# Conditioning weights by input rows, input tiles in three banks, low parts on GpSimd

## The reference, cut to what matters

```
mod = silu(c) @ ada_w + ada_b                      # ada_w 1024 x 6144, c: 9 rows
sh1, sc1, g1, sh2, sc2, g2 = split(mod, 6)
h = rms_norm(x) * (1 + sc1) + sh1
z = h @ w_in                                        # 1024 x 1792
u_pool, v_conv, g_conv, x_lru, g_lru = split(z)
o_pool = pool_mixer(u_pool)                         # running means, then a 64 x 64 product per group
o_conv = silu(layer_norm(depthwise_conv31(v_conv * sigmoid(g_conv))))
xc = conv4(x_lru); r, i = sigmoid(xc @ wa + ba), sigmoid(xc @ wx + bx)
a = exp(-8 r softplus(-lam)); s = scan(a, sqrt(1 - a^2) * i * xc); o_lru = s * gelu(g_lru)
x = x + g1 * (concat(o_pool, o_conv, o_lru) @ w_out)
h2 = rms_norm(x) * (1 + sc2) + sh2
x = x + g2 * moe(h2)                                # top 4 of 32 experts, three 1024 x 1024 matrices each
y = rms_norm(x)
```

## Time and profile before

| | us |
|---|---|
| median of 3 runs (lowest to highest) | 1331.99 (1330.03 to 1334.34) |
| the profiled execution, its time | 1334.82 |
| its span, first to last instruction | 1333.0 |
| PE busy, share of the span | 1251.9 (94%) |
| DVE, ACT, POOL busy | 284.1, 193.0, 118.8 |
| chain that ended last: PE, DMA, DVE, SP's queue | 81%, 8%, 5%, 3% |
| the experts' products, line 1941, share of that chain | 61% |

### The profile page before, as it was taken

How to read it: one execution, slowest core, us unless ns; L and a number is a source line. 1 busy time by engine, 2 the same in 40 slices (tenths; PEclk the granted TensorE clock), 3 DMA queues, 4 the chain that set the end, 5 groups by cost and what they waited for, 6 DMA issues and landing times.

```text
span 1333.0 us, 18761 instructions
## 1 busy us (share of the span) xinstructions
PE 1251.9 (94%) x7974; PEld 551.4 (41%) x7974; DVE 284.1 (21%) x562; ACT 193.0 (14%) x331; POOL 118.8 (9%) x178
## 2 busy tenths in 40 slices
PE   5889979959999999999999999999999999999976
PEld 2758847723333333333333333333333333333322
DVE  2643874673010000010000000001010010001027
ACT  3515251210000000000000000000001001000021
POOL 2011042010100000000001000000000001000000
PEclk9989979959999999999999999999999999999978
DMA  9647278399999999999999999999999999999973
GB/s 362 188 130 254 95 280 272 152 398 386 359 422 421 420 421 422 409 408 410 417 410 420 421 415 420 421 420 394 415 422 419 422 421 421 421 422 421 421 293 151
DMA packets 92004, 486.42 MB, mean 365 GB/s; under 512 B 13649, under 2 KB 21852, under 8 KB 41206
## 3 DMA queue, kind: packets, MB, share of 16 engines
q1 hardware_dynamic: 82451, 462.04, 86.3%
q0 software_dynamic: 8608, 20.82, 4.2%
q10 hardware_dynamic: 859, 2.32, 0.4%
HBM read 470.26 MB, written 18.04 MB: 366 GB/s over the span
## 4 chain that ended last, share of the span: by engine, by line
PE 81%; DMA 8%; DVE 5%; SPq 3%; ACT 1%; issue 1%; POOL 1%; ACTq 0%; DVEq 0%; POOLq 0%
PE psum L1941 61%; DMA raw<-in_moe_w_down 4%; PE psum L1593 4%; PE psum L1588 2%; PE psum L1589 2%; PE psum L1590 2%; SPq L518 2%; PE psum L1931 2%; PE psum L1760 1%; DMA cvs<-in_conv_dw 1%; PE psum L1656 1%; PE psum L2062 1%; DMA raw<-in_ada_w 1%; PE psum L1935 1%; POOL w_lo L687 1%
## 5 line engine op out<-in xcount | busy, mean ns | idle before, releaser
L1941 PE MATMUL psum<-raw,aT 128*64 128x512 f32 (+1 forms) x1728 | 301.2, 533 | 5.1 <-DMA raw<-in_moe_w_down 5.0
L1941 PE MATMUL psum<-raw,xb 128*64 128x512 f32 (+1 forms) x1920 | 304.6, 514 | 0.0
L1941 PE MATMUL psum<-raw,xa 128*64 128x512 f32 x1280 | 283.5, 595 | 0.0
L1514 DVE TENSOR_SCALAR act_t<-psum 128x512 f32<-128x512 f32 (+1 forms) x46 | 28.4, 642 | 874.7 <-PE psum L1941 874.7
L1941 PEld LDWEIGHTS psum<-raw,xb 128*64 128x64 f32 (+1 forms) x1920 | 100.6, 126 | 189.1 <-issue 176.7
L1941 PEld LDWEIGHTS psum<-raw,aT 128*64 128x64 f32 (+1 forms) x1728 | 98.3, 129 | 188.9 <-issue 166.7
L1941 PEld LDWEIGHTS psum<-raw,xa 128*64 128x64 f32 x1280 | 88.2, 137 | 169.7 <-issue 169.4
L701 POOL DMA_INDIRECT xrow<-h_scratch,gidx x24 | 27.4, 1143 | 464.1 <-PE psum L1593 430.0
L999 ACT ACTIVATE glu<-psum 128x512 f32<-128x512 f32 (+1 forms) x46 | 24.3, 559 | 291.8 <-PE psum L1941 291.8
L1588 PE MATMUL psum<-hT_hi,w_hi 128*128 128x260 f32 x208 | 59.4, 285 | 0.0
L1589 PE MATMUL psum<-hT_lo,w_hi 128*128 128x260 f32 x208 | 58.9, 283 | 0.0
(11 more groups left out here) (403 smaller groups left out, 912.6 us busy)
## 6 DMA issues: line engine op xcount, KB each, us to landing
raw<-in_moe_w_gate SPq DMA_DIRECT2D x128, 1024.0 KB, 26.2
raw<-in_moe_w_up SPq DMA_DIRECT2D x128, 1024.0 KB, 26.4
raw<-in_moe_w_down SPq DMA_DIRECT2D x128, 1024.0 KB, 27.1
raw<-in_ada_w SPq DMA_DIRECT2D x24, 1024.0 KB, 7.6
raw<-in_w_in SPq DMA_DIRECT2D x7, 1024.0 KB, 12.4
x<-in_x_prompt SPq DMA_DIRECT2D x2, 2048.0 KB
raw<-in_w_out SPq DMA_DIRECT2D x4, 1024.0 KB, 12.8
yrow_a<-y_scratch SPq DMA_DIRECT2D x2, 2048.0 KB, 10.6
```

The costliest lines, as they stand in the source:

```text
L1514: v.tensor_scalar(act_t[:, b, 0:bank.shape[1]], bank, 8.0, -6.0, ALU.min, ALU.max).then_inc(u_done, 1)
L1941: last = mm(out[w * g4:w * g4 + w, :], x, weights[:, 8 * w * g4:8 * w * g4 + 8 * w], start=start, stop=stop)
```

## The change

A mod chunk is now 128 input rows by 2048 columns, so that each partition reads one run of 8 KB instead of four runs of 2 KB. Eight chunks make one half (g1 and sh2, then 1 + sc2 and g2), which is summed in bank 3, in four strips of 32 partitions, over the whole time of those eight chunks. The 16 chunks are spread between all input tiles, where before 4 came after the fourth pair and 12 after the last. The results leave in two steps, one a half, with eight DMAs of 2 KB rows instead of 32. The input tiles use banks 0 to 2, two neighbours sharing bank 1, where before two pairs took banks 0 to 3. The gates 0 and 1 stand right behind the convolution, in front of the fourth pair of tiles. `lru_out` becomes `lru_mul`, which only multiplies; the high parts of all eight output tiles are made at the end, and the low parts of five of them and of three chunks of `w_out` by POOL (before: two chunks, no output tiles). `ng2` moves into `adab` as 2 loads instead of 8.

```diff
-USE = ([("ada", i) for i in range(ADA_A)] + [("in", i) for i in range(4)] + [("mod", i) for i in range(4)]
...
+USE = (span_of("ada", 0, ADA_A) + span_of("in", 0, 3) + span_of("mod", 0, 4) + span_of("in", 3, 1) + span_of("mod", 4, 4)
...
@@ SP
+            load_piece("mod", 0)
+            sp.wait_ge(zeroed, 2)
...
+            load_piece("mod", 1)
+            for q in range(2):
+                load_late(ng2[32 * q:32 * q + 32, :], norm2_g[:, 512 * q:512 * q + 512].to_broadcast([32, 512]))
+            load_piece("mod", 2)
             sp.wait_ge(mix_done, 1)
@@ POOL
-            for n in range(8):
-                if n in (4, 5):
-                    g.wait_ge(ada_sc, n - 3)
-                else:
-                    g.wait_ge(ada_ev, 5 + n if n < 4 else 3 + n)
+            for h in range(2):
+                g.wait_ge(ada_ev, 5 + h)
+                if h:
+                    g.wait_ge(ada_sc, 1)
                 for j in range(4):
...
+                    g.dma_start(mod_d[:, q], modst[32 * j:32 * j + NC, :]).then_inc(mod_out[h], 16)
-            for c in C_OUT[2:4]:
+            def lo(c):
...
+            lo(C_OUT[0])
+            lo(C_OUT[1])
+            for i, (kk, src) in enumerate(POOL_SPLITS):
+                g.wait_ge(o_hi, i + 1)
+                g.tensor_tensor(oT[:, :, 1, kk, :], by_tile(src)[0], oT[:, :, 0, kk, :].bitcast(F32), ALU.subtract)\
+                    .then_inc(o_split, 1)
+            lo(C_OUT[3])
@@ ACT
+            gates(0)
+            gates(1)
+            roots(0)
+            roots(1)
+            evict(3, (0,))
...
             evict(6)
             gates(2)
             gates(3)
             roots(2)
             roots(3)
             hi(C_OUT[0])
+            mod_rows(1)
             hi(C_OUT[1])
             hi(C_OUT[2])
             hi(C_OUT[3])
@@ DVE
+            lru_mul(2)
+            lru_mul(3)
+            scale_rows()
+            lo(C_OUT[2])
+            dve.wait_ge(lru_made, 4)
+            dve.wait_ge(pool_in, 2)
+            for kk, src in POOL_SPLITS[0:4]:
+                o_high(kk, src, src[:, SEQ:TOK])
+            for m in range(4):
+                o_high(4 + m, x_lru[:, m, :], lru_s[:, m, :])
+            o_low(6, 5, x_lru[:, 1, :])
+            o_low(7, 6, x_lru[:, 2, :])
+            o_low(8, 7, x_lru[:, 3, :])
@@ PE
+            def mods(first, count):
+                for i in range(first, first + count):
+                    h, k = divmod(i, KC)
+                    if k == 0:
+                        pe.wait_ge(ada_ev, 4 + h)
...
             z_tiles(1)
             z_tiles(2)
+            mods(0, 3)
             convolve(0)
             convolve(1)
+            gates(0)
+            mods(3, 1)
+            gates(1)
             z_tiles(3)
...
             channel_sums(4, 6).then_inc(mu_ps, 1)
-            z_tiles(5)
+            mods(4, 4)
+            z_tiles(4)
             pe.wait_ge(sq_done, 2)
             channel_sums(6, 8).then_inc(ln_var, 1)
+            mods(8, 3)
+            z_tiles(5)
+            pool_mix(0)
+            pool_mix(1)
+            mods(11, 2)
             z_tiles(6)
             gates(2)
+            mods(13, 1)
             gates(3)
+            mods(14, 2)
...
-            pe.wait_ge(o_split, 4)
-            pe.wait_ge(oT_done, 4)
+            pe.wait_ge(o_split, 5)
+            pe.wait_ge(oT_done, 3)
```

More of the change, by code:

```diff
@@ L39, with span_of @@
 WOUT = 4
-USE = ([("ada", i) for i in range(ADA_A)] + [("in", i) for i in range(4)] + [("mod", i) for i in range(4)]
-       + [("in", i) for i in range(4, WIN)] + [("mod", i) for i in range(4, ADA_B)] + [("out", i) for i in range(WOUT)])
+def span_of(kind, first, count):
+    return [(kind, i) for i in range(first, first + count)]
+USE = (span_of("ada", 0, ADA_A) + span_of("in", 0, 3) + span_of("mod", 0, 4) + span_of("in", 3, 1) + span_of("mod", 4, 4)
+       + span_of("in", 4, 1) + span_of("mod", 8, 3) + span_of("in", 5, 1) + span_of("mod", 11, 2) + span_of("in", 6, 1)
+       + span_of("mod", 13, 3) + span_of("out", 0, WOUT))
 NO = {piece: n for n, piece in enumerate(USE)}
@@ L109 @@
 WIN_ORDER = [1, 2, 3, 5, 0, 4, 6]
-SLOT = ([0, 1, 2, 3, 4, 5, 6, 7] + [0, 1, 2, 3] + [2, 5, 6, 7] + [4, 0, 1]
-        + [3, 5, 6, 7, 2, 4, 0, 1, 5, 6, 7, 1] + [3, 2, 4, 0])
-LOADS = [("mod", i) for i in range(13)] + [("out", 0), ("mod", 13), ("mod", 14), ("out", 1), ("out", 2), ("mod", 15), ("out", 3)]
+SLOT = ([0, 1, 2, 3, 4, 5, 6, 7] + [0, 1, 2] + [4, 0, 1, 2] + [3] + [5, 6, 7, 2] + [4] + [3, 5, 6] + [0] + [7, 2] + [1]
+        + [5, 6, 7] + [4, 3, 2, 0])
+LOADS = (span_of("mod", 3, 1) + span_of("in", 4, 3) + span_of("mod", 4, 9) + span_of("out", 0, 2) + span_of("mod", 13, 3)
+         + span_of("out", 2, 2))
 STACK_SLOTS = (5, 6, 7)
@@ L473, in _, with load_piece @@
[L473 to L476, removed]
+            def load_piece(kind, c):
+                if kind == "mod":
+                    src = ada[:, c % 8:c % 8 + 1, 2048 * (1 + c // 8):2048 * (2 + c // 8)]
+                elif kind == "in":
+                    src = win[:, :, 256 * WIN_ORDER[c]:256 * WIN_ORDER[c] + 256]
+                else:
+                    src = wout[:, 4 * (c % 2):4 * (c % 2) + 4, (c // 2) * 512:(c // 2 + 1) * 512]
+                load(NO[kind, c], src)
@@ new lines, in _ @@
+            for i in range(4):
+                load_piece("in", i)
+            sp.wait_ge(chunk_used, STACK_SLOTS[0] + 1)
+            load_late(st_lru[:, :], state_lru_conv[0].rearrange("b r c -> (b r) c"))
+            load_late(st_h[:, :], state_lru_h[0])
+            load_late(st_pool[:, :], state_pool[0].rearrange("b r c -> (b r) c"))
+            for a in range(2):
+                load_late(st_conv[:, a, :], state_conv[0, 4 * a:4 * a + 4].rearrange("b r c -> (b r) c"))
+            load_piece("mod", 0)
@@ L477, in _ @@
+            assert late[0] == LATE_LOADS
+            load_piece("mod", 2)
             sp.wait_ge(mix_done, 1)
@@ L483, in _ @@
             for kind, c in LOADS:
[L484 to L485 removed]
+                load_piece(kind, c)
             sp.wait_ge(chunk_used, C_OUT[0])
@@ L911, in _ @@
             evict(1)
-            hi(C_IN[4])
             evict(2)
@@ L934, in _ @@
                           bias=cols[:, LNEPS:LNEPS + 1]).then_inc(ln_sd, 1)
+            evict(5, (0,))
+            for m in range(2):
+                act.wait_ge(ln_pre, m + 1)
+                ac.activation(W[:, 8 + m, :], W[:, 6 + m, :], ACT.Tanh, scale=0.5).then_inc(ln_sig, 1)
+            evict(5, (1,))
+            for m in range(2):
+                act.wait_ge(pool_ps, m + 1)
+                ac.activation(two(sg_conv[:, m, :]), pair(4 + 2 * m), ACT.Copy, scale=cvp(34, m)).then_inc(pool_in, 1)
             evict(6)
@@ L937, in _ @@
             gates(3)
-            for m in range(2):
-                act.wait_ge(ln_pre, m + 1)
-                ac.activation(W[:, 8 + m, :], W[:, 6 + m, :], ACT.Tanh, scale=0.5).then_inc(ln_sig, 1)
             roots(2)
             roots(3)
[L943 to L947, removed]
             hi(C_OUT[0])
+            mod_rows(1)
             hi(C_OUT[1])
-            ada_rows(6)
             hi(C_OUT[2])
-            ada_rows(7)
             hi(C_OUT[3])
             act.wait_ge(tail_ps, 1)
-            act.wait_ge(o_split, 4)
-            act.wait_ge(oT_done, 4)
+            act.wait_ge(o_split, 5)
+            act.wait_ge(oT_done, 3)
             ac.activation(tail[0:23, 0:256], bk[0][0:23, 0:256], ACT.Copy)
@@ L1716, in z_tiles @@
                         pe.wait_ge(z_ev, z - 1)
-                    if z == 9:
-                        pe.wait_ge(ada_ev, 6)
-                    for h in range(2):
-                        out = psum[:, 2 * (z % 2) + h, 0:TOK // 2]
+                    for h in ((0, 1), (1, 0))[z % 2]:
+                        if h == 1 - z % 2:
+                            pe.wait_ge(z_ev, z)
+                        out = psum[:, z % 2 + h, 0:TOK // 2]
                         q = slice(TOK // 2 * h, TOK // 2 * h + TOK // 2)
```

223 lines of the change are left out of this document (89 added, 134 removed).

## The result

The changed kernel takes 1359.53 us, median of three runs (1358.76 to 1359.76), against 1331.99: the ratio is 1.0204, 95% interval 1.0183 to 1.0225, so 2% slower, 27.5 us. Predicted were 1352, range 1340 to 1362.

What follows compares the result with a forecast made beforehand. PE's busy experts' stage was taken to pass on any delay of the projection's first row tile, with GpSimd's list bounding the exit. That tile's +16.2 and 3.8 for DVE-GpSimd overlap gave +20.0: 1332.0 to 1352, range 1340 to 1362.

Steps and rivals of the forecast that it cites:

- rival 1: Exit to the projection: DVE and GpSimd fully exclude each other, +16.2 and 8 to 12, 1356 to 1360; chance 0.22.
- The stall and the gap: Sample states' transposes wait 5.5 for late loads; PE's idle gap at 83 fills; convolution ends at 108.9 instead of 103.4.
- The half clock: Second pair of input tiles: PE runs at half clock after the new stall, +2.5.
- The filled gap: Ahead of the convolution: three mod chunks, about 3.6, fill PE's idle 83 to 87, so it keeps its clock, -2.5.
- The rival without a stall: At 58: small loads overtake the megabyte, 3.5 of stall and 2.5 of clock go, 1346; chance 0.13.
- From the convolution to the last input tile: PE's stretch grows from 57.9 by 9.5 to 67.4; the last input tile ends at 176.3, 15.0 later.
- The recurrence's end: Behind the last input tile: gates 3 done at 181.4, third root at 186.4, DVE's scaled rows at 195.7.
- GpSimd's exit: Behind the scaled rows: issues 2.05, two w_out low parts 9.16, five output-tile low parts 6.0; PE starts at 212.9, 14.5 later.
- DVE and GpSimd at once: Behind the scaled rows: DVE's 9.2 beside GpSimd's 15.2 costs 0 to about 12; 3.8 taken.
- the upper end: Exit overlap: taking turns adds 7; GpSimd's last chunk going ahead of DVE's three low parts makes it about 12.
- first row tile: Output projection: busy 11.7 plus half-clock start, 14.5; done at 227.4 against 211.2, +16.2.
- PE sets the end: Ahead of the projection: PE's idle and weight waits go, projection starts at 185.3, 13 earlier, 1319; chance 0.05.

Runs made afterwards that it cites:

- run 1: Changed kernel with the gain's two small loads issued ahead of mod chunk 1 instead of behind it; 1350.4 us, ratio 1.0151.
- run 2: Changed kernel with the output tiles' eight pairs of copy and cast on ACT instead of DVE; 1355.1 us, ratio 1.0183.
- run 3: Changed kernel with the output tiles' copies and casts still on DVE but written as two-input maxima; 1360.65 us, ratio 1.0229.
- run 8: Changed kernel, gain's loads first, no GpSimd low parts, pairs on ACT, some w_out parts brought forward, last gates around the last input tiles; 1323.1 us, ratio 0.9946.
- run 9: run 2 plus a GpSimd wait, after its second w_out low part, until DVE has made its three low parts; 1352.2 us, ratio 1.0154.
- run 4: Changed kernel with GpSimd's first two w_out low parts ahead of the second half's four writes instead of behind; 1356.9 us, ratio 1.0201.

## Why the prediction was right, and where not

The direction and the range held, but the size came by another way than the forecast's. 1359.5 lies above its own 1345 to 1357 and where rival 1, full exclusion, had put it, at 1356 to 1360. The runs show full exclusion, but that the time fits so well is in part luck: 3.4 of it are scaled rows that came later than predicted, for other reasons.

*The stall and the gap.* 5.5 was put down, 5.87 measured, released by the gain's load. The half clock is the row 65.40:70.40; it cost 2.8 against run 1, where 2.5 was put down. The filled gap kept its clock, as said: the convolution took 13.94 at 1.00, against 16.4 in the earlier trace rows. The rival without a stall is out. The convolution ended at 110.9 instead of 108.9; 1.3 of this lies before the stall, as the first pair ended at 59.6 in this execution (58.3 to 59.4 in the others), and 0.7 is the stall's and the clock's.

*From the convolution to the last input tile.* 67.4 against 68.0.

*The recurrence's end.* The third root was to end 5 behind gates 3. Gates 3 ended at 184.3 and DVE took the root up at 190.16, 5.8 behind. ACT's timeline shows why:

```profile
182.20 1.28 ACT L902 ACT_TABLE_LOAD   x1
183.49 0.82 ACT L902 ACTIVATE g_lru<-W,cols 128x520 f32<-128x520 f32 x1
184.34 0.82 ACT L903 ACTIVATE W<-W,cols 128x520 f32<-128x520 f32 x1
185.20 0.69 ACT L899 ACTIVATE W<-psum,cols 128x520 f32<-128x520 f32 x1
...
189.49 1.16 ACT L914 ACTIVATE W<-W 128x520 f32<-128x520 f32 x2
```

ACT was still at gates 2, with a table load, an exp and a tanh, and came to gates 3 at 185.20, 0.9 late. The sum let it start at once. The load is not new; ACT's timeline before has it in the same place:

```profile
165.58 1.28 ACT L878 ACT_TABLE_LOAD   x1
```

The scaled rows ended at 199.1 instead of 195.7: 2.6 from the later last input tile, 0.8 net from the rest. (The row given for gates 2, at 114.90, is that of gates 0; gates 2 took 1.9 too, from 161.28.)

*GpSimd's exit.* Issues 2.06 and chunks 8.96, as said; the low part of a tile, for which no row existed, takes 1.25 alone (run 2), where the estimate was 1.2.

*DVE and GpSimd at once: the term that was mis-sized.* The prediction took 3.8 between 0 and 12, nearer to the row of a cast at 0.49, and gave full exclusion 0.22. That row was the wrong neighbour: GpSimd was issuing DMAs beside it. And the DVE instructions of the kinds in question are not nine, as rival 1 counts, but twenty: four low parts, eight copies and eight casts. In the changed kernel, too, DVE's low part of w_out takes its usual 2.29 at 199.15 beside GpSimd's issues from 199.65; what shuts DVE out is GpSimd computing. Had each run alone, GpSimd's five parts would have ended at 201.72 + 8.96 + 6.1 = 216.8; PE began at 225.44, so the price is 8.6. The third chunk went ahead of DVE's last pair and its three low parts, as the upper end said. This 4.8 more, and 3.4 from the later scaled rows, less 1.3 for a first row tile of 13.2 instead of 14.5, is most of the 7.4 from +20.0 to +27.4; the rest is the 0.5 from the scaled rows' end to GpSimd's first issue. The rule of the Trainium skill's page SBUF — State Buffer, section Who interferes with whom, gave the better price, 7 to 12: runs 2 and 3 show two inputs held as copies are, for 19.4 and 9.34.

*PE sets the end.* It didn't. Its price, 13 earlier, was about the right size for what lies there: run 8, with GpSimd out of the way and the last gates earlier, starts 11.4 ahead of the kernel before, at 186.99 where the rival had 185.3; by the medians it gains 8.7.

## What to carry to other kernels

Before moving elementwise work from DVE to GpSimd, look at what DVE does at that time: in these runs a GpSimd operation that reads two SBUF tiles and a DVE copy, cast or operation of two SBUF tiles held each other off, so the slower engine's duration was added and not hidden. Other kinds of operations were not tried. ACT took the copies without a conflict. A small load that a wait covers belongs ahead of any load whose slot comes free late. This stage's exit was shortened by work brought forward into DVE's idle time, and not by dividing the work that is left between two engines that hold each other off.

## What the runs showed that was not expected

- A held DVE instruction can wait through many GpSimd instructions: 19.4 through eight in a row (run 2), and it came in after two chunks once GpSimd had a semaphore to wait for (run 9). But a pause isn't always needed: in run 4 it came in between two ready chunks, and in the changed kernel behind each of GpSimd's five low parts, ahead of the third chunk too (218.4), whose high part was ready at 198.3. When it does is left open.
- An instruction of eight columns is held as one of 512 is, until a GpSimd instruction ends (9.34 in run 3, 8.9 in run 9, both over two chunks), so the order of small copies matters as much as that of large ones.
- ACT's copy into fp32r beside GpSimd's chunk, which began at 200.34, took 0.61 in run 2, the same as those ahead of the chunk:

```profile
198.41 0.61 ACT L981 ACTIVATE oT<-sg_conv 128x512 fp32r<-128x512 f32 x1
...
200.89 0.61 ACT L981 ACTIVATE oT<-x_lru 128x512 fp32r<-128x512 f32 x1
```
